# Gated delta recurrence: the 4x4 diagonal blocks of a triangular inverse move from TensorE to VectorE

## What is computed

```
L  = where(strict, (k*beta) @ k.T * decay, 0)          # 64x64 a chunk, strictly lower
T  = solve_triangular(eye + L, eye)                    # (I + L)^-1
u  = T @ (v*beta);  w = T @ (k*beta*exp(g))
for chunk: v_new = u - w @ S
           o     = (q*exp(g)) @ S + (q @ k.T * decay) @ v_new
           S     = S*exp(g_last) + kd.T @ v_new
```

## Time and profile before

| | us |
|---|---|
| median of 3 runs | 2009.96 (2009.28 to 2010.83) |
| the profiled execution, its own time | 2010.26 |
| its span, first to last instruction | 2008.5 |
| PE busy | 1982.9 (99%) |
| DVE busy | 1451.0 (72%) |
| ACT busy | 603.3 (30%) |
| POOL busy | 348.9 (17%) |

### The profile page before, as it was taken

How to read it: one execution, slowest core, us unless ns; L and a number is a source line. 1 busy time by engine, 2 the same in 40 slices (tenths; PEclk the granted TensorE clock), 3 DMA queues, 4 the chain that set the end, 5 groups by cost and what they waited for, 6 DMA issues and landing times.

```text
span 2008.5 us, 31639 instructions
## 1 busy us (share of the span) xinstructions
PE 1982.9 (99%) x12854; PEld 1595.8 (79%) x12854; DVE 1451.0 (72%) x2209; ACT 603.3 (30%) x1045; POOL 348.9 (17%) x317
## 2 busy tenths in 40 slices
PE   9999999999999999999999999999999999999999
PEld 7888888887777777778888877777888888888887
DVE  6666766667876777767998887676666779859973
ACT  2000122222555545423884234574310010000000
POOL 2112111111101011011111212111122212222221
PEclk9999999999999999999999999999999999999999
DMA  5333322322212122222222433221233333333332
GB/s 183 96 93 105 90 83 91 88 91 64 94 57 64 54 68 72 65 64 84 65 74 84 123 94 88 65 63 55 73 94 95 105 94 99 101 95 94 95 100 89
DMA packets 53361, 173.38 MB, mean 86 GB/s; under 512 B 6464, under 2 KB 6720, under 8 KB 53088
## 3 DMA queue, kind: packets, MB, share of 16 engines
q1 hardware_dynamic: 48112, 161.33, 26.5%
q10 hardware_dynamic: 5104, 10.03, 1.8%
HBM read 169.17 MB, written 2.16 MB: 85 GB/s over the span
## 4 chain that ended last, share of the span: by engine, by line
PE 84%; DVE 10%; ACT 3%; issue 2%; DMA 1%; ACTq 0%; DVEq 0%; SPq 0%
PE ps_lin L1935 24%; PE ps_lin L1937 23%; PE ps_lin L1936 23%; PE ps_att L1984 6%; PE ps_aux L1984 4%; DVE arena L439 3%; ACT arena L1350 2%; DVE arena L433 2%; PE ps_att L1993 2%; DVE w_lo L433 1%; DVE arena L436 1%; ACT L1356 1%; PE ps_lin L1955 1%; DVE y_lo L433 0%; PE ps_lin L1957 0%
## 5 line engine op out<-in xcount | busy, mean ns | idle before, releaser
L1935 PE MATMUL ps_lin<-xw_hi,w_hi 128*128 128x512 f32 x1704 | 689.8, 405 | 0.8 <-DVE w_lo L433 0.5
L1937 PE MATMUL ps_lin<-xw_hi,w_lo 128*128 128x512 f32 x1704 | 665.8, 391 | 0.0
L1936 PE MATMUL ps_lin<-xw_lo,w_hi 128*128 128x512 f32 x1704 | 664.9, 390 | 0.0
L415 POOL TENSOR_SCALAR w_hi<-raw 128x1024 fp32r<-128x1024 f32 (+2 forms) x309 | 345.0, 1117 | 1641.5 <-PE ps_lin L1937 1522.2
L1350 ACT ACTIVATE arena<-arena 128x512 f32<-128x512 f32 (+7 forms) x328 | 202.1, 622 | 713.1 <-DVE arena L433 323.6
L433 DVE TENSOR_TENSOR w_lo<-raw,w_hi 128x1024 fp32r<-128x1024 f32 (+2 forms) x340 | 378.2, 1115 | 45.4 <-POOL w_hi L415 17.5
L1937 PEld LDWEIGHTS ps_lin<-xw_hi,w_lo 128*128 128x128 f32 x1704 | 320.3, 188 | 68.6
L1935 PEld LDWEIGHTS ps_lin<-xw_hi,w_hi 128*128 128x128 f32 x1704 | 320.8, 188 | 67.5 <-issue 3.5
L1936 PEld LDWEIGHTS ps_lin<-xw_lo,w_hi 128*128 128x128 f32 x1704 | 321.2, 189 | 58.5
L433 DVE TENSOR_TENSOR arena<-ps_lin,rstd 128x512 f32<-128x512 f32 (+3 forms) x220 | 147.7, 671 | 193.5 <-PE ps_lin L1937 185.2
L1935 PE MATMUL ps_lin<-y_hi,w_hi 128*128 128x512 f32 (+1 forms) x544 | 205.3, 377 | 0.0
(11 more groups left out here) (188 smaller groups left out, 1676.0 us busy)
## 6 DMA issues: line engine op xcount, KB each, us to landing
raw<-in_w_up SPq DMA_DIRECT2D x44, 512.0 KB, 3.6
raw<-in_conv_w_in SPq DMA_DIRECT2D x32, 512.0 KB, 3.6
raw<-in_fox_w_in SPq DMA_DIRECT2D x32, 512.0 KB, 3.6
raw<-in_gdn_w_in SPq DMA_DIRECT2D x32, 512.0 KB, 3.6
raw<-in_w_gate SPq DMA_DIRECT2D x24, 512.0 KB, 3.6
raw<-in_swa_w_in SPq DMA_DIRECT2D x20, 512.0 KB, 3.7
raw<-in_w_ml SPq DMA_DIRECT2D x16, 512.0 KB, 3.7
raw<-in_w_down SPq DMA_DIRECT2D x16, 512.0 KB, 3.6
```

Of the source, the lines that this page charges most:

```text
L415: pool.tensor_scalar(w_whole(n, kc * c)[0], w_raw(n, kc * c), 1.0, 0.0, mult, add).then_inc(s("w_rounded"), 1)
L1935: pe.matmul(o, wh, hi, start=first and k == 0, stop=False)
L1936: pe.matmul(o, wh, lo, start=False, stop=False)
L1937: ins = pe.matmul(o, wl, hi, start=False, stop=last and k == kc - 1)
```

## The change

The diagonal blocks that need no doubling grow from 2x2 to 4x4 (`BASE` = 4), and doubling begins at level 2 (`LEVEL0` = 2). DVE inverts the 4x4 blocks itself: it keeps the four columns of all 4x4 blocks in a [128, 4 chunks, 4] tile, gets a lane's three neighbours by `stream_shuffle`, and eliminates column by column. The slots of level 1 go ahead of the levels (`GDN_FILL["U0"]` 3 to 6); generators are chained and no longer run to their end at slots 15, 23 and 31; the sum of squares after slot 15 goes after slot 18.

```diff
-        GDN_FILL = {"tok": 4, "squares": 4, "A": 0, "U0": 3}
+        GDN_FILL = {"tok": 4, "squares": 4, "A": 0, "U0": 6}
-        LAST_PIECE = {1: (0, 0), 2: (1, 0), 3: (2, 0), 5: (0, 1), 6: (1, 1), 7: (2, 1), 8: (0, 2), 9: (1, 2), LAST_FILL: (2, 2)}
-        LAST_PIECE.update({LAST_FILL + at: (3 + i // BANKS, i % BANKS) for i, at in enumerate((1, 2, 4, 5, 7, 8, 9, 11, 14))})
-        LAST_PIECE[LAST_FILL + 20] = (0, BANKS)
+        LAST_PIECE = {1: (0, 0), 2: (1, 0), 3: (2, 0), 5: (0, 1), 6: (1, 1), 7: (2, 1), 8: (0, 2), 9: (1, 2), 10: (2, 2), 12: (3, 0), LAST_FILL: (3, 1)}
+        LAST_PIECE.update({LAST_FILL + at: (3 + i // BANKS, i % BANKS) for i, at in enumerate((1, 2, 4, 5, 6, 8, 11), 2)})
+        LAST_PIECE[LAST_FILL + 17] = (0, BANKS)
+        SQUARES = {18: 1, 3 * ND - 1: 2}
...
DVE, gdn_head
+                step(dve.tensor_copy(F["Ud"], over_chunks(mat("unit_pairs1234")[:, 0:BASE])))
                 dve.wait_ge(s("gdn_A"), 2 * h + 1)
                 dve.wait_ge(s("gdn_decay"), h + 1)
                 step(tt(F["LT"], ps_att[:, 0, :], F["DT"], mult))
...
                 for top in (0, HD):
-                    step(tt(U0[top:top + HD], chunks(F["LT"])[top:top + HD, :, top:top + HD], over_chunks(mat("pairs0_ident")[top:top + HD, 0:HD], HD), mult))
-                step(tt(U0, U0, over_chunks(mat("pairs0_ident")[:, HD:]), add))
+                    last = tt(U0[top:top + HD], chunks(F["LT"])[top:top + HD, :, top:top + HD], over_chunks(own[top:top + HD], HD), mult)
+                step(last)
+                step(dve.tensor_reduce(F["Ld"], U0.rearrange("p c (b j) -> p c j b", j=BASE), AX.X, add))
+                for k in range(BASE - 1):
+                    last = dve.stream_shuffle(F["E"][:, :, k, :], F["Ld"], [i - i % BASE + k for i in range(32)])
+                step(last)
+                for k in range(BASE - 1):
+                    n = BASE - 1 - k
+                    step(tt(F["El"][:, :, 0:n], F["E"][:, :, k, k + 1:], F["Ud"][:, :, k:k + 1].to_broadcast([P, NT, n]), mult))
+                    step(tt(F["Ud"][:, :, k + 1:], F["Ud"][:, :, k + 1:], F["El"][:, :, 0:n], sub))
+                step(tt(U0.rearrange("p c (b j) -> p c b j", j=BASE), F["Ud"].unsqueeze(2).to_broadcast([P, NT, HD // BASE, BASE]),
+                        own.rearrange("p (b j) -> p b j", j=BASE).unsqueeze(1).to_broadcast([P, NT, HD // BASE, BASE]), mult))
                 dve.transpose(F["Tm"][:, 0:NT * HD], F["Uc"]).then_inc(s("gdn_T0"), 1)
                 dve.wait_ge(s("gdn_A"), 2 * h + 2)
                 tt(F["QK"], ps_att[:, 1, :], F["DT"], mult).then_inc(s("gdn_QK"), 1)
...
-                fill(2)
-                fill(2, held=True)
-                for l in range(1, 7):
+                fill(3)
+                fill(GDN_FILL["U0"] + 1 - 3, held=True)
+                for l in range(LEVEL0, 7):
...
-                    if l == 1:
-                        more(1)
-                    else:
-                        fill(1)
+                    fill(1)
...
-                        if l == 1 and h == GDN_H - 1:
+                        if l == LEVEL0 and h == GDN_H - 1:
                             gdn_out_scale(h - 1)
...
-                    if l == 1:
+                    if l == LEVEL0 + 1:
                         more(1)
-                        fill(1)
-                    fill(LEVEL_FILL[l], held=l == 1)
+                    fill(LEVEL_FILL[l])
...
DVE and ACT, fill
-                                for _ in pieces:
-                                    pass
-                                pieces = gdn_tile(r, done // ND)
+                                pieces = itertools.chain(pieces, gdn_tile(r, done // ND))
...
ACT, gdn_head
-                for l in range(1, 7):
+                for l in range(LEVEL0, 7):
                     d = 1 << l
-                    fill(1)
+                    fill(1, held=l == LEVEL0)
+                    if l == LEVEL0 + 2:
+                        more()
...
-                    fill(LEVEL_FILL[l])
+                    fill(LEVEL_FILL[l], held=l == LEVEL0)
...
PE, gdn_head and fill
-                for l in range(1, 7):
+                for l in range(LEVEL0, 7):
...
-                            if r and done[0] % ND == ND - 1:
-                                gdn_tile(r, done[0] // ND)
+                            if r and done[0] in SQUARES:
+                                gdn_tile(r, SQUARES[done[0]])
```

More of the change, by code:

```diff
@@ L10 @@
 from contextlib import ExitStack
+import itertools
 import numpy as np
@@ L32 @@
 RAW, SPLIT, BANKS = 3, 3, 3
+BASE, LEVEL0 = 4, 2
 def stream():
@@ L129 @@
         "window_add", "causal_add"]\
-    + ["before", "pairs0_ident", "pairs1234", "pairs5"]
+    + ["before", "blocks_ident", "unit_pairs1234", "pairs5"]
 MAT = {n: i for i, n in enumerate(MATS)}
@@ L141, in constants @@
     q, f = p % HD, np.arange(HD)[None, :]
-    m["pairs0_ident"] = np.concatenate([-1.0 * ((f % 2 == 1) & (q == f - 1)), 1.0 * (q == f)], axis=1)
+    m["blocks_ident"] = np.concatenate([1.0 * (q // BASE == f // BASE), 1.0 * (q == f)], axis=1)
     def pairs(l):
@@ L147, in pairs @@
         return -1.0 * ((q // (2 * s) == j // s) & (q % (2 * s) >= s))
-    m["pairs1234"] = np.concatenate([pairs(l) for l in range(1, 5)], axis=1)
+    m["unit_pairs1234"] = np.concatenate([1.0 * (q % BASE == f[:, 0:HD // 2])] + [pairs(l) for l in range(2, 5)], axis=1)
     m["pairs5"] = np.concatenate([pairs(5), np.zeros((P, P - HD // 2))], axis=1)
@@ L266, in block_program @@
                    nwT=gdn["LT"], vn=gdn["Tm"], X=[None] + [spare[:, i, :] for i in range(6)], Uc=spare[:, 0, NT * HD:], kbg=spare[:, 6, :], vb=spare[:, 7, :])
+        rows_at, small = NT * (BASE - 1) * BASE, spare[:, 0 if BASE == 4 else 1, 64 if BASE == 4 else 0:]
+        gdn.update(E=spare[:, 0, 0:rows_at].rearrange("p (c k j) -> p c k j", c=NT, j=BASE),
+                   Ld=spare[:, 0, rows_at:rows_at + NT * BASE].rearrange("p (c j) -> p c j", c=NT),
+                   Ud=small[:, 0:NT * BASE].rearrange("p (c j) -> p c j", c=NT), El=small[:, NT * BASE:2 * NT * BASE].rearrange("p (c j) -> p c j", c=NT))
         mem_sq = arena[:, 14 * T:14 * T + ND * MEM]
@@ L409, in _ @@
                 elif ASIDE.get(n) == "gdn_w_out":
-                    pool.wait_ge(s("gdn_T"), 5 * (GDN_H - 2) + 4)
+                    pool.wait_ge(s("gdn_T"), (6 - LEVEL0) * (GDN_H - 2) + 5 - LEVEL0)
                 elif ASIDE.get(n) == "swa_w_out":
@@ L820, in gdn_head @@
                     step(dve.memset(chunks(F["U"])[HD:, :, 0:HD], 0.0))
-                U0 = chunks(F["Uc"])
+                U0, own = chunks(F["Uc"]), mat("blocks_ident")[:, 0:HD]
                 for top in (0, HD):
-                    step(tt(U0[top:top + HD], chunks(F["LT"])[top:top + HD, :, top:top + HD], over_chunks(mat("pairs0_ident")[top:top + HD, 0:HD], HD), mult))
-                step(tt(U0, U0, over_chunks(mat("pairs0_ident")[:, HD:]), add))
+                    last = tt(U0[top:top + HD], chunks(F["LT"])[top:top + HD, :, top:top + HD], over_chunks(own[top:top + HD], HD), mult)
[10 more added lines that the diff above has]
+                        own.rearrange("p (b j) -> p b j", j=BASE).unsqueeze(1).to_broadcast([P, NT, HD // BASE, BASE]), mult))
                 dve.transpose(F["Tm"][:, 0:NT * HD], F["Uc"]).then_inc(s("gdn_T0"), 1)
@@ L856, in gdn_head @@
                             gdn_out_scale(h - 1)
-                        if l == 1 and h == GDN_H - 1:
+                        if l == LEVEL0 and h == GDN_H - 1:
                             gdn_out_scale(h - 1)
-                        if l == 2 and h == GDN_H - 1:
+                        if l == LEVEL0 + 1 and h == GDN_H - 1:
                             step(dve.tensor_copy(y_hi[:, h - 1, :], v_tmp[:]))
-                        if l == 4 and h == GDN_H - 1:
+                        if l == LEVEL0 + 2 and h == GDN_H - 1:
                             tt(y_lo[:, h - 1, :], v_tmp[:], y_hi[:, h - 1, :].bitcast(f32), sub).then_inc(s("y_ready"), 1)
                             dve.wait_ge(s("y_ready"), made("y_ready"))
-                    if l == 1:
+                    if l == LEVEL0 + 1:
                         more(1)
-                        fill(1)
-                    fill(LEVEL_FILL[l], held=l == 1)
+                    fill(LEVEL_FILL[l])
                 fill(1)
@@ L1466, in _ @@
                     act.wait_ge(s("z_silu"), made("z_silu"))
-            for l in range(1, 6):
-                step(act.activation(gdn["X"][l][:, 0:NT * HD].rearrange("p (c t) -> p c t", c=NT), mat("pairs0_ident")[:, HD:].unsqueeze(1).to_broadcast([P, NT, HD]), ACT.Copy))
+            for l in range(LEVEL0, 6):
+                step(act.activation(gdn["X"][l][:, 0:NT * HD].rearrange("p (c t) -> p c t", c=NT), mat("blocks_ident")[:, HD:].unsqueeze(1).to_broadcast([P, NT, HD]), ACT.Copy))
             norm([tile_of("fox_w_out", m) for m in range(ND)])
@@ L1556, in gdn_decay, with gdn_head @@
                     gdn_rows_G(h + 1)
```

(35 more changed lines are left out.)

15 lines of the change are left out of this document (8 added, 7 removed).

## The result

The changed kernel takes 2025.05 us (median of 4 runs, 2024.01 to 2026.28) against 2010.39 (4 runs) for the kernel before: a ratio of 1.0071 with a 95% interval of 1.0058 to 1.0083. It is 14.7 us slower, where 9 us faster was forecast. The profiled execution took 2025.55 us, with a span of 2023.6.

What follows compares the result with a forecast made beforehand. PE, busy 99% of the span, was taken to bound the kernel. Seven heads at 1.52 - 0.6 + 0.3 give 8.5 us, the last head 0.5, together 9.0: 2010.26 - 9.0 = 2001.3 us, range 1996.0 to 2005.5.

Steps and rivals of the forecast that it cites:

- What goes from PE: Level 1's two matmul sets and the tiling-mode changes around them leave PE's queue: 1.52 us saved a head.
- The chain on DVE: DVE's inversion of the 4x4 blocks, from LT to the transpose giving T0: 2.1 us longer than before.
- rival 2: Each DVE shuffle costs 0.45 us, like a 256-element transpose; stall 1.45 us, time 2008.0 us; chance 0.12.
- rival 3: Each DVE shuffle loads its list for 1.28 us; T0 late, stall 4.4 us, time 2031 us; chance 0.06.
- The copy: DVE's copy into Ud before LT: free, or held by POOL's rounding until about 714.60; the second was taken.
- A stall of 0.6 us at X: PE waits before level 2's XU for DVE's X, behind two taps: 0.6 us a head, bounds 0 and 4.
- T0: DVE's inverted blocks, ready at 719.3, in time for PE's XT of level 2 at 719.84, by 0.5 us.
- The end of a head: Before the first recurrence step two taps stand on DVE, not three; the copy comes earlier: 0.3 us gained a head.
- What moves on DVE and ACT: Later tap 2, w_lo halves, Silu, square of q, Uc copy, DMA and table loads: all costed at nothing.

Runs made afterwards that it cites:

- e1: Changed kernel with the q tile's w_lo halves made early (before slot 7's evacuation and in the empty step), one tap behind X: 2001.84 us, ratio 0.9954.
- e6: Kernel before, level 1 kept, six unused operations before X of level 2 and four before the second half of w_lo: 2043.25 us, ratio 1.0158.
- e5: On e2, second half of w_lo moved behind X with five unused operations before it: 2034.30 us, ratio 1.0109.
- e9: e5 with three unused operations before the second half of w_lo in place of five: 2019.13 us, ratio 1.0039.
- e3: Kernel before, level 1 kept, five unused operations before the second half of the q tile's w_lo from round 1: 2023.03 us, ratio 1.0061.
- e2: On e1, all taps behind X of level 2, sum of squares behind slot 19, Silu of q behind ACT's level 2 copy: 2005.65 us, ratio 0.9975.
- e8: On e1, two slots between XT and XU of level 2, and the copy into Ud before slots 4 to 7: 2000.37 us, ratio 0.9949.

## Why the prediction was wrong

By its steps:

- **What goes from PE**, 1.52 us a head: nothing speaks against it, but no run takes level 1 out alone. e1, which has about the prediction's waits, is at 2001.84 against the 2001.3 of the sum. The 768 records went too, and in e1 a head follows the other 41.9 to 42.3 us later (XU of level 2 starts at 591.14, 633.06, 674.97, 716.86, 759.11, 801.13), where 42.0 was said. That the sum is met so closely is in part luck. From the chunk at 530.2 us to the same chunk a round later e1 takes 44.5 us and the kernel before 44.4, so the first head, for which 1.2 us were forecast, gains nothing: T0 is late there. The next six gain 7.9 us together (7.3 forecast) and the last 0.9 (0.5 forecast).
- **The chain on DVE**: right in its sum, 4.77 against 4.7 us. Within it the reduction was dearer (0.61 against 0.43 and a gap) and the shuffles cheaper: three starts 0.09 us apart, the list of each loaded in 0.01 us. So rival 2 and rival 3, the one that ended on the slower side, are out: the slower time did not come by its way. The prediction's estimate of 0.27 us fixed for a shuffle, worked out from the figure in the Trainium skill, VectorE: DVE Perf Modes, Rules for kernel authors, did not show at 16 elements: the whole shuffle takes 0.17. The copy did meet GpSimd's rounding: 0.37 us, and e1 shows 0.40.
- **A stall of 0.6 us at X**: right in place, cause and size: 0.69 in head 3, and in e1 0.9 in the first head and 0.5 in the next six. (The range's upper end, 2005.5, goes with a stall of 1.2 us; the 1.1 that it names gives 2004.7.)
- **T0**: 0.46 us ahead in head 3, as said. That it is late in the first head and the last (1.8 us in all) was not said for the first.
- **The end of a head**: two taps and no late copy; the first step's matmul starts at 705.59, right behind the chunk, where it was 0.25 us late in the earlier trace rows.
- **What moves on DVE and ACT, "I cost all of these at nothing"**: this step failed. It says "The two halves end near 724.8" and only asks who is late on DVE behind them. It never asks who waits for what the halves make. They are the `w_lo` of the v tile, and by the prediction's own times PE wants it at slot 16, 721.75 + 0.68 = 722.43: 2.4 us before. That alone was 7 x 2.4 = 17 us, and would have turned the sign (2010.3 - 9.0 + 17 = 2018). Measured were seven waits of 1.8 to 1.9 us, 13.1 in all. The old code ran the generator to its end at slot 15, behind X; in the new one T and a tap come before, with GpSimd's rounding on top.
- **The clock** was not in the prediction, not even as a rival. In the changed kernel it cost 2.4 to 2.6 us in a long stretch and 1.3 to 1.4 in a short one, some 13 us. e1 against the changed kernel shows the two together: 23.2 us by the medians and 25.3 in the profiled executions, of which 13.1 are the waits for `w_lo`; e1 has small waits of its own (T0 in the first head, the square of q) that take about 2 us off the sum.

So the slower time has two causes of about equal size, and one origin. e1 shows the origin: with `w_lo` early both are gone. That the new mix is not needed for the clock to fall is shown by e6, where it falls with level 1 kept; that the mix alone does not make it fall, by e1; and that longer waits make it fall more often, by e5 and e9. Why it falls after one wait and not after another like it (the first head of the changed kernel against the next six, two of e3's seven rounds, the last head of e2 against that of e1) stays open.

## What to carry to other kernels

When a hand-written order is shifted, list for every step that moves what it produces and the first instruction anywhere that waits for it, the weight pipeline's steps first: they look like filler but have a hard date. Where PE is 99% busy, price a wait of some 2 us at more than itself: where the clock fell with it, that cost 1.3 to 2.6 us more. And repair by moving the dated step ahead into idle time, before taking out any arithmetic.

## What the runs showed of the hardware

- The granted clock fell from 2.4 to 1.2 GHz, for 3.4 or 6.8 us at a time. At the falls PE had waited 2.6 us in one piece (e5, seven rounds of seven), or 0.7 and 1.9 us with 0.7 us of 32x32 matmuls between (the changed kernel, heads 1 to 6), or 1.6 and 1.7 us (e6, seven of seven); in some of these the fall came just before the last wait ended. At 1.7 us for `w_lo` it fell in two rounds of seven in e3 and in one in e9, where a wait of 1.25 us for T0 went before. It did not fall in the first head of the changed kernel, after 0.65, 1.08 and 1.81 us, and never in the stage in e1, whose waits are 0.9 us at most but for T0's (1.2). So no single length of wait parts the cases. I had taken a wait on TensorE to cost its own length.
- STREAM_SHUFFLE of 128x16 takes 0.17 us and three without waits start 0.09 us apart, each with its own list. TENSOR_REDUCE of 256 elements to 16 took 0.61 us where an addition over 256 takes 0.43.
- A copy of 16 elements beside GpSimd's rounding takes 0.37 to 0.40 us, and away from it 0.17 us (e8).
